# Compressed blocks of a two-block transformer: another form of the first layer's matmuls, and another accumulator bank for the gates

## What is computed

```python
def compress(kv, pos, w1, w2, n_cmp):
    idx = jnp.arange(n_cmp)[:, None] * CMP_STRIDE + jnp.arange(CMP_LEN)[None, :]
    blk = kv[:, idx] + pos[None, None, :, None, :]
    blk = blk.transpose(0, 3, 1, 2, 4).reshape(B, N_KV_HEADS, n_cmp, CMP_LEN * HEAD_DIM)
    return jax.nn.gelu(blk @ w1) @ w2
...
    proj = n @ w_in[l]
    k_cmp = compress(kvh(k_c), cmp_pos_k[l], cmp_w1_k[l], cmp_w2_k[l], n_cmp)
    v_cmp = compress(kvh(v_c), cmp_pos_v[l], cmp_w1_v[l], cmp_w2_v[l], n_cmp)
...
    br_gates = jax.nn.sigmoid(g_br).reshape(B, S, N_NSA_BRANCHES, N_HEADS)
```

## Time and profile before

| | us |
|---|---|
| median of 3 runs | 815.16 |
| lowest and highest run | 813.63, 816.73 |
| the profiled execution | 819.39 |
| its span, first to last instruction | 817.7 |
| TensorE busy / weight loads busy | 770.2 / 723.6 |
| DVE / ACT / POOL busy | 519.8 / 397.3 / 73.1 |
| mean share of full clock granted to TensorE | 0.987 |

### The profile page before, as it was taken

The page is one execution under the profiler, slowest core; times in us unless marked ns, Lnnn a source line. Parts: engine busy times, 40 slices in busy tenths (PEclk is TensorE's granted clock), DMA queues, the critical chain, the costliest instruction groups (busy, mean ns, idle before and its releaser), DMA issues.

```text
span 817.7 us, 13827 instructions
## 1 busy us (share of the span) xinstructions
PE 770.2 (94%) x5693; PEld 723.6 (89%) x5693; DVE 519.8 (64%) x886; ACT 397.3 (49%) x711; POOL 73.1 (9%) x106
## 2 busy tenths in 40 slices
PE   2989999999999998999999998898988999999998
PEld 2989999999989987999899987897867999889996
DVE  5655565766654767776456646677877776446662
ACT  4345665545455435554344545468554545435440
POOL 8000000014022001000000003300500000000000
PEclk9989999999999999999999999999999999999999
DMA  9866746333433464565665551733334655655521
GB/s 283 220 202 206 204 99 175 116 103 105 155 104 130 155 206 142 194 194 173 201 201 162 204 181 52 230 115 146 103 112 123 205 187 199 194 183 190 169 90 51
DMA packets 108414, 132.12 MB, mean 162 GB/s; under 512 B 4267, under 2 KB 97513, under 8 KB 108352
## 3 DMA queue, kind: packets, MB, share of 16 engines
q1 hardware_dynamic: 106048, 126.56, 48.6%
q0 software_dynamic: 2304, 4.68, 2.5%
HBM read 129.39 MB, written 1.84 MB: 160 GB/s over the span
## 4 chain that ended last, share of the span: by engine, by line
PE 57%; DVE 8%; ACT 3%; issue 2%; POOL 1%; ACTq 0%; DVEq 0%; POOLq 0%
PE B L1419 34%; PE B L1435 21%; DVE LO L891 3%; DVE X L1136 1%; POOL SGC L463 1%; DVE NW L907 0%; DVE AL L897 0%; ACT HI L508 0%; PE B L1573 0%; DVE TMP L1339 0%; ACT SGC L819 0%; DVE TOK L1140 0%; DVE NW L909 0%; ACT AH L512 0%; ACT PT L516 0%
## 5 line engine op out<-in xcount | busy, mean ns | idle before, releaser
L891 DVE TENSOR_TENSOR LO<-RAW,HI 128x1024 fp32r<-128x1024 f32 x240 | 283.8, 1216 | 116.8 <-ACT HI L508 116.6
L1419 PE MATMUL B<-AH,HI 128*128 128x256 f32 x1200 | 347.5, 290 | 10.8 <-DVE SGA L949 4.3
L1419 PE MATMUL B<-AL,HI 128*128 128x256 f32 x1200 | 342.9, 286 | 0.0
L1419 PE MATMUL B<-AH,LO 128*128 128x256 f32 x1200 | 342.6, 285 | 0.0
L508 ACT ACTIVATE HI<-RAW 128x1024 fp32r<-128x1024 f32 x240 | 237.6, 1039 | 65.5 <-PE B L1435 59.8
L1419 PEld LDWEIGHTS B<-AH,HI 128*128 128x128 f32 x1200 | 232.7, 194 | 14.1 <-DVE SGA L949 4.5
L1419 PEld LDWEIGHTS B<-AL,HI 128*128 128x128 f32 x1200 | 232.9, 194 | 0.4
L1419 PEld LDWEIGHTS B<-AH,LO 128*128 128x128 f32 x1200 | 232.7, 194 | 0.1
L1435 PE MATMUL B<-HI,AH 128*128 128x512 f32 (+1 forms) x400 | 141.3, 353 | 8.0 <-DVE LO L891 4.2
L1435 PE MATMUL B<-LO,AH 128*128 128x512 f32 (+1 forms) x400 | 139.9, 350 | 0.0
L1435 PE MATMUL B<-HI,AL 128*128 128x512 f32 (+1 forms) x400 | 139.8, 349 | 0.0
(11 more groups left out here) (274 smaller groups left out, 597.3 us busy)
## 6 DMA issues: line engine op xcount, KB each, us to landing
RAW<-in_w_in SPq DMA_DIRECT2D x30, 1024.0 KB, 5.7
RAW<-in_w_gate SPq DMA_DIRECT2D x22, 1024.0 KB, 5.3
RAW<-in_w_up SPq DMA_DIRECT2D x22, 1024.0 KB, 5.3
RAW<-in_w_down SPq DMA_DIRECT2D x22, 1024.0 KB, 5.0
RAW<-in_w_in SPq DMA_DIRECT2D x9, 512.0 KB, 5.6
RAW<-in_w_attn_out SPq DMA_DIRECT2D x4, 1024.0 KB, 5.0
RAW<-in_w_o SPq DMA_DIRECT2D x4, 1024.0 KB, 5.0
RAW<-in_w_out SPq DMA_DIRECT2D x4, 1024.0 KB, 5.0
```

What stands on the lines that cost most here:

```text
L891: e.tensor_tensor(pieces(LO, NSPL, i, k), pieces(RAW, NRAW, i, k), pieces(HI, NSPL, i, k), ALU.subtract).then_inc(split_lo, 1)
L1419: x = e.matmul(dst, w[:, t, c0:c0 + n], a, start=(t == 0 and k == 0), stop=(t == nk - 1 and k == 2))
```

## The change

It has two parts.

The gates' product is written to bank 2 instead of bank 1, and the tanh reads it there. Bank 1 is next used by the queries.

In the hidden layer the weights become the stationary operand and the inputs move. The high and low parts of the inputs lie side by side, 60 columns each (`XB`; the keys' two parts in `AH[12:20]`, the values' in `AL[12:20]`). For each of the 16 pieces and each of the two halves of 128 hidden units, one matmul takes the weights' high part and moves 120 columns (both parts), and one takes the weights' low part and moves the 60 high columns. The result in the bank is 128 hidden units by 2 x (60 + 60). DVE copies the second 60 of each out to the new tile `HX` and adds the first 60; the gelu then runs from `HX` in `HT`, which already has the form that the second layer reads. The two transposes for each of keys and values, and ACT's copies of them, are gone; their factor 0.5 is applied in the copies behind the second layer.

```diff
@@ buffers
+        HX = sb("HX", [128, 2, 2, 60])
...
+        XB = [v[:, 12:20, :].rearrange("p a b -> p (a b)")[:, 0:1920].rearrange("p (l b n) -> p l b n", b=2, n=60)
+              for v in (AH, AL)]
@@ ACT
-            e.activation(TMP[0:48, 0, 0:S], B[1][0:48, 0:S], ACT.Tanh, scale=0.5).then_inc(gates_tanh, 1)
+            e.activation(TMP[0:48, 0, 0:S], B[2][0:48, 0:S], ACT.Tanh, scale=0.5).then_inc(gates_tanh, 1)
...
-                hid = TMP[0:60, kv, 0:256]
-                e.wait_ge(hid_pe, 2 * kv + 2)
-                if kv == 0:
-                    e.wait_ge(gturn_pe, 1)
-                e.activation(hid, B[kv][0:60, 0:256], ACT.Square).then_inc(hid_act, 1)
-                e.wait_ge(hid_dve, 2 * kv + 1)
+                hid = HT[:, kv, :, :]
+                e.wait_ge(hid_dve, 3 * kv + 1)
+                e.activation(hid, HX[:, kv, :, :], ACT.Square).then_inc(hid_act, 1)
+                e.wait_ge(hid_dve, 3 * kv + 2)
                 e.activation(hid, hid, ACT.Tanh, scale=math.sqrt(2.0 / math.pi)).then_inc(hid_act, 1)
@@ DVE
-                hid, x = TMP[0:60, kv, 0:256], B[kv][0:60, 0:256]
+                hid, x = HT[:, kv, :, :], HX[:, kv, :, :]
+                parts = B[kv][:, 0:240].rearrange("p (c b n) -> p c b n", c=2, b=2)
+                e.wait_ge(hid_pe, 2 * kv + 2)
+                e.tensor_copy(x, parts[:, :, 1, :]).then_inc(hid_low, 1)
+                e.wait_ge(hid_low, kv + 1)
+                e.tensor_tensor(x, parts[:, :, 0, :], x, ALU.add).then_inc(hid_dve, 1)
                 e.wait_ge(hid_act, 2 * kv + 1)
@@ TensorE
-            take(1, gates_tanh, 1)
-            stationary(U_GATES, 0, B[1][0:48, 0:S], 0, True, n=48).then_inc(gates_pe, 1)
+            take(2, gates_tanh, 1)
+            stationary(U_GATES, 0, B[2][0:48, 0:S], 0, True, n=48).then_inc(gates_pe, 1)
...
-                        c = slice(60 * (8 * half + t), 60 * (8 * half + t) + 60)
-                        for k, (a, w) in enumerate(((hi, wh), (hi, wl), (lo, wh))):
-                            x = e.matmul(B[kv][0:60, 0:256], a[:, c], w[:, t, :], start=(half == 0 and t == 0 and k == 0),
-                                         stop=(half == 1 and t == 7 and k == 2))
+                        for c in range(2):
+                            dst, w = B[kv][:, 120 * c:120 * c + 120], slice(128 * c, 128 * c + 128)
+                            first, last, x = half == 0 and t == 0 and c == 0, half == 1 and t == 7 and c == 1, XB[kv][:, 8 * half + t]
+                            e.matmul(dst, wh[:, t, w], x, start=first, stop=False)
+                            x = e.matmul(dst[:, 0:60], wl[:, t, w], x[:, 0, :], start=False, stop=last)
                     x.then_inc(hid_pe, 1)
             for kv in range(2):
-                e.wait_ge(hid_dve, 2 * kv + 2)
-                take(5 + kv, hturn_sb, kv + 1)
-                for c in range(2):
-                    x = e.transpose(B[5 + kv][:, 60 * c:60 * c + 60], TMP[0:60, kv, 128 * c:128 * c + 128], ident[0:60, 0:60])
-                x.then_inc(hturn_pe, 1)
                 values(U_VALS, 0, kv)
-            e.wait_ge(hturn_sb, 2)
+            e.wait_ge(hid_dve, 6)
```

More of the change, by code:

```diff
@@ L158, in program @@
         q_pe, q_sb = sem("q_pe"), sem("q_sb")
-        hid_pe, hid_act, hid_dve = sem("hid_pe"), sem("hid_act"), sem("hid_dve")
-        hturn_pe, hturn_sb = sem("hturn_pe"), sem("hturn_sb")
+        hid_pe, hid_low, hid_act, hid_dve = sem("hid_pe"), sem("hid_low"), sem("hid_act"), sem("hid_dve")
         ck_pe, ck_sb, cv_pe, cv_sb = sem("ck_pe"), sem("ck_sb"), sem("cv_pe"), sem("cv_sb")
@@ L546, in block_high @@
                 e.wait_ge(block_sb, 2 * kv + 2)
-                e.activation(flatten(AH[:, 12 + 4 * kv:16 + 4 * kv, :])[:, 0:960], flatten(src[:, 0:4, :])[:, 0:960],
+                e.activation(XB[kv][:, :, 0, :], flatten(src[:, 0:4, :])[:, 0:960].rearrange("p (l n) -> p l n", n=60),
                              ACT.Copy).then_inc(block_hi, 1)
@@ L568, in _ @@
                 hi(U_HID + 2 * kv + 3)
-                hid = TMP[0:60, kv, 0:256]
-                e.wait_ge(hid_pe, 2 * kv + 2)
-                if kv == 0:
-                    e.wait_ge(gturn_pe, 1)
-                e.activation(hid, B[kv][0:60, 0:256], ACT.Square).then_inc(hid_act, 1)
-                e.wait_ge(hid_dve, 2 * kv + 1)
-                e.activation(hid, hid, ACT.Tanh, scale=math.sqrt(2.0 / math.pi)).then_inc(hid_act, 1)
[L577 to L582, removed]
+                hid = HT[:, kv, :, :]
+                e.wait_ge(hid_dve, 3 * kv + 1)
+                e.activation(hid, HX[:, kv, :, :], ACT.Square).then_inc(hid_act, 1)
+                e.wait_ge(hid_dve, 3 * kv + 2)
+                e.activation(hid, hid, ACT.Tanh, scale=math.sqrt(2.0 / math.pi)).then_inc(hid_act, 1)
             hi(U_VALS + 2)
             values(0, 0)
-            turned_hidden(1)
             values(0, 1)
@@ L592, in _ @@
                              B[0][r, 0:60].rearrange("p (c h n) -> p c h n", c=2, h=2)[:, :, half, :],
-                             ACT.Copy).then_inc(ck_sb, 1)
+                             ACT.Copy, scale=0.5).then_inc(ck_sb, 1)
             e.wait_ge(cv_pe, 1)
@@ L597, in _ @@
                 e.activation(VB[32 * j:32 * j + 15, :, 64 * j:64 * j + 64],
-                             B[1][0:15, 0:256].rearrange("p (g d) -> p g d", g=4), ACT.Copy).then_inc(cv_sb, 1)
+                             B[1][0:15, 0:256].rearrange("p (g d) -> p g d", g=4), ACT.Copy,
+                             scale=0.5).then_inc(cv_sb, 1)
             e.wait_ge(rel_pe, 1)
@@ L954, in block_low @@
                 e.wait_ge(block_hi, kv + 1)
-                c = slice(12 + 4 * kv, 16 + 4 * kv)
-                e.tensor_tensor(flatten(AL[:, c, :])[:, 0:960], flatten(src[:, 0:4, :])[:, 0:960],
-                                flatten(AH[:, c, :])[:, 0:960], ALU.subtract).then_inc(block_lo, 1)
+                e.tensor_tensor(XB[kv][:, :, 1, :], flatten(src[:, 0:4, :])[:, 0:960].rearrange("p (l n) -> p l n", n=60),
+                                XB[kv][:, :, 0, :], ALU.subtract).then_inc(block_lo, 1)
             block_sums(0, SGC, 0)
@@ L1480, in _ @@
             for kv in range(2):
-                hi, lo = (flatten(v[:, 12 + 4 * kv:16 + 4 * kv, :])[:, 0:960] for v in (AH, AL))
-                take(kv, hid_dve, 2 * kv + 2)
+                take(kv, hid_dve, 3 * kv + 1)
                 e.wait_ge(block_lo, kv + 1)
```

## The result

The changed kernel takes 822.3 us in the median (820.7 to 825.4) against 815.0 us before: 1.0093 times as long, 95% interval 1.0056 to 1.013. It is 7.3 us slower, where 4.5 us faster was forecast. The profiled execution took 825.4 us.

A forecast was written before the change was run, and what follows sets the result against it. TensorE, busy for 770.2 of 817.7 us, was taken as the bound. Terms of -6.5 (gates), +3.1 (hidden layer) and -1.1 (turns) summed to -4.5 us, from 815.2 to 810.7, range 809.0 to 819.0.

The forecast's parts named there:

- The gates' bank: Gates to third query product: writing to bank 2 removes TensorE's idling and the clock drop there, -6.5 us.
- ACT's stall: Before the third query product: TensorE waits 0.2 us for ACT's copy of the first query product to free bank 0.
- The pace of the new matmuls: Hidden layer: loading 128 weight columns sets the pitch, 112 ns a matmul.
- +3.1 - 1.1 of the sum: Hidden layer's 128 matmuls for 96 cost +3.1 us; dropping the four turns and their waits before the values gives -1.1.
- the multiplication by 128: Hidden layer: 128 matmuls at 0.112 us each make 14.3 us instead of 11.24, +3.1.
- Rival B: Clock falls in the hidden layer, doubling the loads to 28.2 us; sum +10, 825 us in all; chance 0.13.
- the decision point of 0.294 us a pair: Hidden layer: the price of a pair at which the whole change turns from gain to loss.
- The row at 15.62 us: Transposes with a pitch of 217 ns instead of 107, read as showing that loads double at half clock.
- Rival A: Hidden layer: narrow fp32r runs below full rate, 0.32 us a pair, +9.4; sum +1.8, 817.0 us; chance 0.28.
- Rival C: Query products: ACT, DVE or a transfer is 2 us late, so the early gain isn't all carried; -2.5, 812.7; chance 0.10.
- Rival D: Hidden layer: weight loads overlap, 82 ns a matmul, -0.7; sum -8.3, 806.9 us; chance 0.04.
- The figure of 81 ns a pair: The skill's price per load-and-matmul at 128 columns: hidden layer 10.4 us, a gain of 0.9; set aside for the trace's rows.

The follow-up runs named there:

- the bank alone: The kernel before with the gates in bank 2 and nothing else: 809.0 us against 816.4 (0.9903), then 807.7 against 814.6 (0.9907).
- The profile with 480 columns: The changed kernel with each matmul moving 240 columns (inputs repeated), 480 a pair instead of 180: 810.1 us against 816.4, ratio 0.9921.
- the run with halves: The kernel before with the gates in bank 2 and each 256-column hidden-layer matmul cut into two of 128: 809.3 us in one run.
- The kernels with more columns: The changed kernel moving 240, 480 or 210 columns a pair instead of 180: 811.1, 810.1 and 810.6 us (210 again: 810.4).

## Why the prediction was wrong

- **The gates' bank** was right: no idling, 117 ns a matmul, clock at 1.00, third query product at 48.46 (48.55 forecast), hidden layer at 65.53 (65.9). The term was -6.5 and measured -6.9 in the profile, -6.7 between the landmarks of the bank alone and -7 in its runs. ACT's stall was the right next limit, and its size too: the third product started 0.42 us after the turns (48.04), 0.17 more than before. The profile with 480 columns names ACT at this place, with a longer stall:

```profile
47.09 0.38 PE L1417 MATMUL B<-AH,HI 128*128 128x256 f32 x1 [0.37 <-ACT QT L567]
```

- **The pace of the new matmuls** was right: 223 ns a pair against 224, at full clock. Its reason was right too, the load of 128 columns (the run with halves). With the clock held, the layer and the values took from 64.16 to 83.97, 19.8 us, where the forecast had 14.3 + 5.74 = 20.0; against 18.07 us for the bank alone that is the +3.1 - 1.1 of the sum, +2.0 forecast and +1.7 measured. The kernels with more columns are 5.0 to 5.2 us shorter than before in the distance and 4.2 to 6.3 us faster in the runs, where the forecast was 4.5. That they also ended at 810 to 811, like the forecast of 810.7, is partly luck: the kernel before ran at 816.4, 816.3 and 814.6 us beside them, not at the 815.2 of the sum.
- **The step that failed is the multiplication by 128**: it took the pitch of the first matmuls for all of them, that is, a clock at 1.00 for 14 us of matmuls that move 180 columns in 224 ns. Rival B had this mechanism, its place and its reason, and the decision point of 0.294 us a pair, which the mean of 23.38/64 = 0.365 us passed. But it stood at 0.13, and the range left it out. The only row that spoke against it (16 narrow loads that left the clock alone) covered 1.9 us, and the clock fell 4.1 us into the layer. The row that spoke for it, the fall at 243.4 after sparse work with 1.7 us of idling, was taken for a case of idling.
- **Rival B's size** was +10 and measured +6.1 in the profile, +7.3 in the runs: the first 4.1 us ran at full clock (37 of 128 matmuls), so the layer took 23.38 us and not 28.2; from the layer to `W2K` it took 2.0 us more than the forecast, not 1. The row at 15.62 us that B read as half clock has a granted clock of 1.00 in the windows (10 to 20 us). That loads slow down with the clock is shown by the changed kernel (333 ns, 213 ns a matmul), not by that row.
- **Rival A** fell. No price of narrow fp32r but the load's shows at 60, 90, 120, 128 or 240 columns. **Rival C** fell, the early gain was all carried. **Rival D** fell: the pitch with loads of full height stayed at 112 ns and did not come to 82.
- Two small slips in the working change nothing: (54.59 - 48.96)/47 is 119.8 ns, and the range starts at 809.0, though the lowest bound of the sum is 809.8.

The figure of 81 ns a pair, from the Trainium skill's "TensorE: Matmul & The Clock Gate", section "Back-to-back issue gap", is not what these runs show for fp32r: 111.5 ns with 60 to 240 moved columns. The Trainium skill's section "LDWEIGHTS (loading the stationary operand)", on the same page, has a load's time as its columns by 1.2 GHz; worked out from that, as an estimate, it is 107 ns for 128 columns and 50 for 60. At full clock the measured pitches of 112 and 60 ns are not in conflict with it, with some handover on top. At the low clock the pitch is: it was 213 ns, so here the load follows the granted clock.

## What to carry to other kernels

Count a matmul by two numbers: its weight columns, which set the pace here when few columns moved, and its moved columns per time, with which the clock stayed up or fell in these kernels. An exchange of moved columns for weight columns can lose both ways, though the sum of columns falls. In a narrow stretch of several microseconds it is worth trying to widen the moving operand up to what the load hides: here a pair with 480 columns took 224 ns, and one with 180 took 223 at the same clock, and the kernel went from 7.3 us slower than before to 6.3 faster. And a wait in front of a small product can be worth more than its length: 4.3 us of idling, with the half clock behind it, cost 7 us, and another free bank removed it.

## What the hardware showed that was not expected

- The clock fell from 2.4 to 1.2 GHz with TensorE at 4.00 of 4.00 us busy and no idle time in any row, 4.1 us into a stretch of pairs that moved 180 columns in 223 ns (3.8 us with the gates in bank 1), and stayed low for 23.9 us, until the values' wide matmuls had run for 4.6 us. With 210, 240 and 480 columns in 222 to 224 ns it did not fall. The Trainium skill ("TensorE: Matmul & The Clock Gate", section "HAM oscillation — how this bites in real kernels") gives idle gaps as the cause; this run had none in that stretch. The fall at the gates of the kernel before, at about 42.0 us in the 4.3 us of idling, agrees with it.
- A load of 128 weight columns took 192 ns at the full clock and 333 at half, and the pitch that it sets went from 112 to 213 ns.
- fp32r matmuls of 60 to 240 moved columns with 128 weight columns all had a pitch of 111 to 112 ns; with 60 weight columns and 128 moved it was 60.5.
